# Start addresses of TensorE's operands: moving tiles at multiples of 1024 bytes, weight halves 64 bytes past a multiple of 512

## What is computed

```python
# first block (one layer)
h = rmsnorm(x, attn_norm_g)
proj = h @ w_in                               # 1024 x 3080: q, k, v of both kinds, forget logits
o = concat(rmsnorm(fox_attention(...)), rmsnorm(stick_breaking_attention(...)))
x = x + o @ w_out                             # 1024 x 1024
u = causal_dwconv(rmsnorm(x, ffn_norm_g) @ w_up, conv_w, conv_b)   # 1024 x 5632
x = x + (silu(gate) * val) @ w_down           # 2816 x 1024
x = rmsnorm(x, final_norm_g)
# second block, layers i = 0, 1
mod = silu(c) @ w_ada[i] + b_ada[i]           # 1024 x 6144, six vectors
h = rms_norm(x, norm_mix[i]) * (1 + sc_m) + sh_m
y = attention(h) @ w_o  if i == 0  else  short_conv(h)
x = x + g_m * y
h = rms_norm(x, norm_ffn[i]) * (1 + sc_f) + sh_f
x = x + g_f * (silu(h @ w_gate) * (h @ w_up)) @ w_down
```

## Time and profile before

| | |
|---|---|
| median of 3 runs | 913.37 us |
| lowest, highest | 910.86, 913.92 us |
| span of the profiled execution | 909.7 us |
| TensorE busy | 900.3 us (99%), 7367 matmul records |
| VectorE busy | 749.3 us (82%) |
| ScalarE busy | 503.3 us (55%) |
| granted TensorE clock | full speed in all 40 slices |
| transfers | 207.7 MB, mean 228 GB/s |

### The profile page before, as it was taken

One profiled execution on the slowest core, in us unless ns is written; L12 is line 12 of the kernel. 1 busy time (PEld: TensorE's weight loads), 2 busy tenths in 40 slices (PEclk: granted clock), 3 DMA queues, 4 the chain that ended last, 5 costly groups with the idle time before them and its releaser, 6 DMA issues.

```text
span 909.7 us, 18262 instructions
## 1 busy us (share of the span) xinstructions
PE 900.3 (99%) x7367; PEld 875.8 (96%) x7367; DVE 749.3 (82%) x1032; ACT 503.3 (55%) x776; POOL 49.5 (5%) x87
## 2 busy tenths in 40 slices
PE   8999999999999999999999999999999999999998
PEld 7999999999999989999999999999999999999886
DVE  6999989999899789898987887987998887667544
ACT  6446757666665467764754444436645564444531
POOL 5100000000001000010000100100000000000000
PEclk9999999999999999999999999999999999999999
DMA  9887375666667947575469988984687467664541
GB/s 288 281 282 270 115 244 197 220 222 207 231 232 278 325 137 255 169 268 192 139 205 325 335 301 314 328 268 149 199 280 260 139 229 251 235 213 180 186 139 47
DMA packets 132129, 207.71 MB, mean 228 GB/s; under 512 B 4711, under 2 KB 109537, under 8 KB 126945
## 3 DMA queue, kind: packets, MB, share of 16 engines
q1 hardware_dynamic: 123968, 156.47, 51.3%
q0 software_dynamic: 8064, 50.34, 15.9%
q10 hardware_dynamic: 32, 0.01, 0.0%
HBM read 205.75 MB, written 1.05 MB: 227 GB/s over the span
## 4 chain that ended last, share of the span: by engine, by line
PE 91%; DVE 5%; ACT 2%; issue 1%; DMA 1%; SPq 0%; ACTq 0%; DVEq 0%
PE bank L1673 25%; PE bank L1675 25%; PE bank L1674 25%; PE bank L1828 2%; PE bank L1744 2%; PE bank L1753 2%; PE bank L1742 2%; PE bank L1710 1%; PE bank L1718 1%; PE bank L1712 1%; DVE w_lo L1002 1%; DMA w_raw<-in_w_in 1%; ACT w_hi L582 1%; PE bank L2028 0%; PE bank L2157 0%
## 5 line engine op out<-in xcount | busy, mean ns | idle before, releaser
L1002 DVE TENSOR_TENSOR w_lo<-w_raw,w_hi 128x1024 fp32r<-128x1024 f32 x294 | 353.8, 1221 | 107.6 <-ACT w_hi L582 105.4
L582 ACT ACTIVATE w_hi<-w_raw 128x1024 fp32r<-128x1024 f32 x293 | 306.1, 1056 | 242.3 <-PE bank L1675 226.7
L1673 PE MATMUL bank<-act_hi,w_hi 128*128 128x256 f32 x1312 | 366.1, 279 | 0.1
L1675 PE MATMUL bank<-act_hi,w_lo 128*128 128x256 f32 x1312 | 363.0, 277 | 0.0
L1674 PE MATMUL bank<-act_lo,w_hi 128*128 128x256 f32 x1312 | 363.0, 277 | 0.0
L1673 PEld LDWEIGHTS bank<-act_hi,w_hi 128*128 128x128 f32 x1312 | 246.5, 188 | 0.7 <-issue 0.6
L1674 PEld LDWEIGHTS bank<-act_lo,w_hi 128*128 128x128 f32 x1312 | 246.6, 188 | 0.4 <-issue 0.2
L1675 PEld LDWEIGHTS bank<-act_hi,w_lo 128*128 128x128 f32 x1312 | 246.6, 188 | 0.0
L1018 DVE SCALAR_TENSOR_TENSOR ada_acc<-ada_raw,silu_c,ada_acc 128x2048 f32<-128x2048 f32 (+1 forms) x56 | 114.3, 2040 | 1.7 <-DMA ada_raw<-in_w_ada 1.4
L1673 PE MATMUL bank<-hid_hi,w_hi 128*128 128x256 f32 x352 | 98.2, 279 | 0.0
L1674 PE MATMUL bank<-hid_lo,w_hi 128*128 128x256 f32 x352 | 97.2, 276 | 0.0
(11 more groups left out here) (309 smaller groups left out, 1374.0 us busy)
## 6 DMA issues: line engine op xcount, KB each, us to landing
w_raw<-in_w_gate_up SPq DMA_DIRECT2D x44, 1024.0 KB, 5.2
ada_raw<-in_w_ada POOLq DMA_DIRECT2D x40, 1024.0 KB, 5.3
w_raw<-in_w_down SPq DMA_DIRECT2D x33, 1024.0 KB, 5.1
w_raw<-in_w_in SPq DMA_DIRECT2D x23, 1024.0 KB, 6.8
w_raw<-in_w_up SPq DMA_DIRECT2D x22, 1024.0 KB, 5.7
w_raw<-in_w_qkv SPq DMA_DIRECT2D x12, 1024.0 KB, 7.3
w_raw<-in_w_out SPq DMA_DIRECT2D x8, 1024.0 KB, 7.0
ada_raw<-in_w_ada POOLq DMA_DIRECT2D x16, 512.0 KB, 4.9
```

The costliest lines, as they stand in the source:

```text
L582: act.activation(unit(w_hi, u), raw_half(c, h), ACT.Copy).then_inc(hi_ready, 1)
L1002: dve.tensor_tensor(unit(w_lo, u), raw_half(c, h), unit(w_hi, u).bitcast(F32), ALU.subtract).then_inc(lo_ready, 1)
L1673: pe.matmul(dst, a_hi, b_hi, start=start, stop=False, skip_group_check=True)
L1675: return pe.matmul(dst, a_lo, b_hi, start=False, stop=stop, skip_group_check=True)
```

## The change

It changes the order of declarations and nothing else: no instruction is added, taken away or moved, and no size changes. `mod`, `silu_c` and `silu_e` (448 bytes together) go ahead of `w_hi`; `gain2`, `rowsum`, `nmax` and `q_rstd` (448 bytes) go between `res` and `act_hi`. `rinv`, `nlf`, `fold` and `stack` leave the permanent part and are laid into a phase of their own, above 70 x 256 elements (71,680 bytes) that keep them clear of the other phases' tiles.

```diff
@@ -119,21 +119,23 @@
         w_raw = sb("w_raw", [P, RAW, 2 * UNIT])
+        mod = sb("mod", [P, 2, 6 * KT])
+        silu_c = sb("silu_c", [P, KT])
+        silu_e = sb("silu_e", [P, KT])
         w_hi = sb("w_hi", [P, SPLIT, UNIT], F32R)
         w_lo = sb("w_lo", [P, SPLIT, UNIT], F32R)
         res = sb("res", [P, KT, T])
-        mod = sb("mod", [P, 2, 6 * KT])
-        silu_c = sb("silu_c", [P, KT])
-        silu_e = sb("silu_e", [P, KT])
+        gain2 = sb("gain2", [P, 4, KT])
+        rowsum = sb("rowsum", [P, 16, 2])
+        nmax = sb("nmax", [P, 16, 2])
+        q_rstd = sb("q_rstd", [P, 4, 4])
         act_hi = sb("act_hi", [P, KT, T], F32R)
         act_lo = sb("act_lo", [P, KT, T], F32R)
         ada_raw = sb("ada_raw", [P, 2, ADA_W])
         ada_acc = sb("ada_acc", [P, 3, ADA_W])
         vec = sb("vec", [P, 4, P])
-        gain2 = sb("gain2", [P, 4, KT])
         qk_gain = sb("qk_gain", [P, 1])
         q_rms = sb("q_rms", [P, 3, 4])
-        q_rstd = sb("q_rstd", [P, 4, 4])
@@ -145,17 +147,18 @@
         before = sb("before", [P, 2, P])
-        rowsum = sb("rowsum", [P, 16, 2])
-        nmax = sb("nmax", [P, 16, 2])
-        rinv = sb("rinv", [P, 16, 2])
         small = sb("small", [P, 4, 8])
         wf_two = sb("wf_two", [P, KT, 16], F32R)
         f_bias = sb("f_bias", [P, 8])
         x_rms = sb("x_rms", [P, 6, 2])
-        nlf = sb("nlf", [P, 2, 8])
         f_cum = sb("f_cum", [P, 2, 8])
-        fold = sb("fold", [P, P])
-        stack = sb("stack", [P, 32])
+        phase = ExitStack()
+        phase.enter_context(nc.sbuf_tensor("below_top", [P, 70 * T], F32))
+        fold = sb("fold", [P, P], stack=phase)
+        stack = sb("stack", [P, 32], stack=phase)
+        rinv = sb("rinv", [P, 16, 2], stack=phase)
+        nlf = sb("nlf", [P, 2, 8], stack=phase)
+        phase.close()
```

## The result

The changed kernel takes 921.94 us (median, 921.82 to 930.86) against 913.29 us of the kernel before (910.86 to 913.92). The ratio of the executions is 1.0126, with a 95% interval of 1.010 to 1.0152: slower by about 1.3%, where 888.4 us had been forecast. The profiled execution spans 919.9 us, 10.2 more than that of before. Executions with a lower granted clock (934.6 us at 0.95 and 1515.5 us at 0.56, in later rounds) are left out of every comparison.

A forecast was written before the change was run, and what follows sets the result against it. The prediction took TensorE's spacing of matmuls to bound the kernel. From the profiled 909.7 us it took 25 us for aligned moving rows and added 3.7 us to reach the median, giving 888.4 us, range 876 to 917.

The forecast's parts named there:

- What bounds the kernel: Whole kernel: TensorE, busy 900.3 of 909.7 us, sets the time through how far apart matmuls start; waits some 5 us.
- The two forms, 113 and 118: fp32r matmuls of 256 columns step at 113.3 ns, or 117.5 to 117.7 ns where small attention matmuls interrupt the stream.
- What loses time is the moving tile when it goes through at full rate: fp32r matmuls: reading the moving tile costs 6.7 ns beyond the pure 106.7 ns for 256 columns.
- The row on narrow weights: Profile row with 16 or 8 weight columns, 117 ns a step; read as showing weight load size is not what costs.
- Step 1: Price of an aligned moving row of 256 fp32r columns: 109.3 ns, bounded by 106.7 below and 113.3 or 117.7 above.
- step 3: Sum over TensorE's matmuls: 20.6 us from steady ones and 5.0 us from slow ones, together 25.6 us saved.
- The extra cost of 258 columns: Matmuls of 258 columns step at 120.7 ns, 13.2 over 107.5; taken as reads going in pieces, each touched piece paid.
- Step 2: Count of the 256-column matmuls whose moving rows become aligned: 5832, of them 5150 steady and 600 slow.
- The new weight offset at nothing: Weights going from 128 to 576 past a multiple of 1024 priced at zero, bounds 4.4 ns per matmul either way.
- Step 4: What is late next: VectorE from 140 to 255 us and transfers keep up; 0.6 us off for stalls, leaving 25 us.
- Nothing changes: Rival for the whole kernel, 913 us, chance 0.27: the loss comes with full-rate reading, wherever the row begins.
- Slower: Rival for the long loops, 936 us, chance 0.14: new places of moving rows and weights bring the slow form, 22.7 us.

The follow-up runs named there:

- `offsets`: Separate kernel without the model: streams of 48 fp32r matmuls at twelve pairs of moving and weight offsets, plus other widths; 256 columns stepped at 113.3 to 120.0 ns.
- `w_only`: Kernel before with only the weight halves moved, from 128 to 576 past a multiple of 1024; 945.86 us, 1.0376 times the kernel before.
- `m_only`: Changed kernel with mod, silu_c and silu_e put back behind res, so only moving tiles move and weights stay at 128; 940.22 us, 1.0323.
- `offsets2`: Separate stream kernel without the model: every multiple of 16 bytes of distance, narrower weights, more widths, varied preceding float32 operands; 256 columns stepped at 113.3 to 120.4 ns.
- `kick_after`: Changed kernel plus one float32 matmul of 64 columns before the long stream in each of three feed-forward layers; 918.11 us, 1.0074 times the kernel before.

## Why the prediction was wrong

- *What bounds the kernel*: right. TensorE is busy for 99% of the span in every version, and each span is its stream's steps added up: 919.9, 945.5, 926.6 and 918.8 us come out of counts times 4.44 or 6.67 ns to within 1 us.
- *The two forms, 113 and 118*: right in the numbers, and put too low in rank. The prediction read them as a matter of the short stretches that attention interrupts. They are two ways in which every stream seen at distance 192 runs, and a long stream keeps the one with which it starts over 1391 steps. The loops of before were not steady for a reason of their own; they had entered well.
- *"What loses time is the moving tile when it goes through at full rate"*: this is where the forecast failed. The row on narrow weights was read as freeing the weight load of all blame. It has 16 and 8 columns of weights and a step of 117, not 113 ns; at 128 columns the step turned out to be 113.3 to 120.0 ns by where the weights begin against the moving tile. The row showed that few weights do not help, and was taken to show that the place of many does not matter.
- *Step 1, 109.3 ns for an aligned row*: wrong. Measured at offset 0: 113.3 ns (885 records in 100 us, mean 276 ns). This is the term of the sum that fell: the 25.6 us of step 3, all derived from it, were not there. The two rows with 576 and 832 bytes gave the same 113.3 ns, and this was taken as two samples of "unaligned"; they were two samples of distance 192. The extra cost of 258 columns stands (120.9 ns measured alone), but it does not show a boundary of 1024 bytes; 254 columns, 1016 bytes, cross none from such a multiple, and cost 120.0 ns there, more than the 118.3 of 256 columns (`offsets`, distance 128).
- *Step 2, the counts*: 5150 and 600 held; with them `w_only` and `m_only` come out to within 1 us of their spans.
- *The new weight offset at nothing, bounds 4.4 ns either way*: in the change as a whole right, because the moving tiles went along; by itself it costs 6.7 ns per matmul, outside the bounds.
- *Step 4*: no wait at `w_lo` appeared, as there was no gain to cause one.
- *Nothing changes*: right for the moving tiles' address as such, and it is the whole result with the constants 64 bytes further on (912.4 us).
- *Slower*: this is what came, in the terms in which it was stated, the long loops going over into the slower form, from 610 matmuls on. It was 2350 of the 5150, hence 10.4 us and not 22.7. What it gave as the cause, the moving rows against the weights, had not changed; the float32 constants against the weights had. No step of the prediction looked at the tiles that are read just before a loop starts, so that it had a case for this outcome (0.14) and not the reason for it.

## What to carry to other kernels

Where TensorE sets the time and its matmuls follow without a gap, look at the steps, not the busy share: a stream can hold one of two paces for over a hundred microseconds, and it is chosen at its entry. Before moving tiles, list the offsets of moving tile, weights and whatever TensorE reads shortly before as differences modulo 256 bytes; absolute alignment did nothing here, a difference did. Look at single executions too: a median can hide that one stream's form changes from one to the next. An edit that only moves addresses should be tried in parts and with a shift of the small tiles by 32 or 64 bytes, because 64 bytes of a constant's place were worth as much as the whole change.

## What the runs showed of the hardware

- The step depends on the distance from the start of the weights to the start of the moving tile: with 256 fp32r columns and 128 of weights, 113.33 or 117.78 ns per matmul at 192 modulo 256 bytes, 120.0 at 0, 118.2 to 120.0 at 128, 117.8 and at times 113.3 at 64, at a granted clock of 1.00 (`offsets`, `offsets2`, `w_only`, `m_only`).
- Moving all tiles by 64 bytes changes nothing (1.0001, 0.9991 to 1.001).
- fp32r matmuls with 128 columns of weights step by about 111.7 ns at least, for 64 columns as for 240, and by 213.3 ns at 1.2 GHz.
- Matmuls of 258 columns run through a cycle of eight steps between 118 and 125 ns, whose place is kept over at least 84 matmuls. One such matmul more or less ahead of a stream can switch its form (`offsets`).
- One float32 matmul of 64 columns ahead of a stream switched its pace to its end (1391 steps at most), to the faster in two places and to the slower in one (`kick_after`).
- The stream of 510 changes its form between executions of one kernel, 2.3 us.
